# Page loads of the compression phase issued from three queues instead of two

## The reference, cut to what matters

```
def _compress(kv_rows, pe_k, w1_k, w2_k, pe_v, w1_v, w2_v, k_norm_g):
    idx = jnp.arange(n_cmp)[:, None] * CMP_STRIDE + jnp.arange(CMP_BLK)[None, :]
    blk = kv_rows[:, idx]
    def phi(x, pe, w1, w2):
        x = (x + pe[:, None, :]).transpose(0, 1, 3, 2, 4).reshape(B, n_cmp, NSA_GROUPS, CMP_BLK * HEAD_DIM)
        return jax.nn.gelu(x @ w1) @ w2
    kc = _rms(phi(blk[:, :, :, 0], pe_k, w1_k, w2_k), k_norm_g)
    vc = phi(blk[:, :, :, 1], pe_v, w1_v, w2_v)
```

## Time and profile before

| | us |
|---|---|
| median of 3 runs | 3017.89 (3014.96 to 3022.27) |
| the profiled execution, its own time | 3013.03 |
| its span in the profile | 3011.3 |
| the compression phase in it | about 463.5 to 704.9 |
| PE idle in that phase, waiting for rows | 14.4, 15.8 and 17.0 |

### The profile page before, as it was taken

One profiled execution on the slowest core, in us unless ns is written; L12 is line 12 of the kernel. 1 busy time (PEld: TensorE's weight loads), 2 busy tenths in 40 slices (PEclk: granted clock), 3 DMA queues, 4 the chain that ended last, 5 costly groups with the idle time before them and its releaser, 6 DMA issues.

```text
span 3011.3 us, 44556 instructions
## 1 busy us (share of the span) xinstructions
PE 2725.2 (90%) x18210; PEld 2239.4 (74%) x18210; DVE 934.6 (31%) x2644; ACT 640.0 (21%) x1615; POOL 482.5 (16%) x461
## 2 busy tenths in 40 slices
PE   7999994798998755997599999999999999999995
PEld 3555534544666544644599999999999999999995
DVE  1122121114766442145422223232322322232222
ACT  1111111114756410022011111111111111111111
POOL 0000002100000000012222313131322321222121
PEclk9999985898999866798799999999999999999997
DMA  5000026200000222321677778888889999999995
GB/s 183 11 21 20 13 92 155 56 0 27 1 1 1 82 74 84 105 84 55 245 245 245 254 262 273 282 285 301 294 294 321 316 313 326 318 322 309 324 317 176
DMA packets 278641, 533.63 MB, mean 177 GB/s; under 512 B 53906, under 2 KB 90226, under 8 KB 278226
## 3 DMA queue, kind: packets, MB, share of 16 engines
q1 hardware_dynamic: 234610, 475.29, 44.5%
q0 software_dynamic: 33120, 46.46, 7.2%
q10 hardware_dynamic: 10704, 9.00, 0.9%
HBM read 492.21 MB, written 42.96 MB: 178 GB/s over the span
## 4 chain that ended last, share of the span: by engine, by line
PE 50%; DMA 1%; DVE 1%; SPq 0%; issue 0%; POOL 0%; POOLq 0%; ACT 0%; DVEq 0%; ACTq 0%
PE up L2030 33%; PE down L2041 17%; DMA w_up<-summed_rows 0%; DMA slot_rows<-slot_tokens_gates 0%; DMA summed_rows<-y_rows,row_index_cur 0%; SPq L1978 0%; POOL summed_rows L1994 0%; PE down L2047 0%; POOLq L1874 0%; DVE nb L2162 0%; DVE hT L2119 0%; DVEq L1939 0%; DVE obt L2168 0%; DVE obt L2173 0%; DVE obf L2169 0%
## 5 line engine op out<-in xcount | busy, mean ns | idle before, releaser
L2030 PE MATMUL up<-hT,w_up 128*128 128x128 f32 (+19 forms) x8192 | 1008.0, 286 | 18.2 <-DVE hT L2119 18.2
L2030 PEld LDWEIGHTS up<-hT,w_up 128*128 128x128 f32 x8192 | 1004.9, 191 | 18.5 <-issue 18.5
L2041 PE MATMUL down<-actT,w_down 128*128 128x128 f32 (+19 forms) x4096 | 508.0, 286 | 0.5 <-DVE actT L2144 0.4
L2041 PEld LDWEIGHTS down<-actT,w_down 128*128 128x128 f32 x4096 | 503.6, 191 | 1.9 <-DVE actT L2144 0.9
L1994 POOL DMA_INDIRECT summed_rows<-y_rows,row_index_cur x153 | 241.0, 1575 | 1086.0 <-ACT y_rows L2060 1049.4
L2139 DVE TENSOR_SCALAR glu<-up,b_up_cur 128x128 f32<-128x128 f32 (+19 forms) x256 | 93.5, 365 | 1021.1 <-PE up L2030 1000.1
L305 PE MATMUL zp<-w_in,xnT 128*128 128x512 f32 (+3 forms) x896 | 366.0, 565 | 1.4 <-DVE xnT L479 1.4
L305 PEld LDWEIGHTS zp<-w_in,xnT 128*128 128x128 f32 (+1 forms) x896 | 156.8, 191 | 185.5 <-issue 181.5
L2071 ACT ACTIVATE sig<-glu 128x128 f32<-128x128 f32 (+19 forms) x256 | 82.4, 322 | 869.0 <-DVE glu L2139 797.0
L2079 ACT ACTIVATE yT<-down,b_down_cur 128x128 f32<-128x128 f32 (+19 forms) x256 | 97.2, 380 | 394.4 <-PE down L2041 394.4
L1988 POOL DMA_INDIRECT x_rows<-h_rows,row_index_cur x153 | 149.8, 979 | 65.1 <-issue 46.0
(11 more groups left out here) (389 smaller groups left out, 2089.6 us busy)
## 6 DMA issues: line engine op xcount, KB each, us to landing
w_up<-in_w_up SPq DMA_DIRECT2D x128, 2048.0 KB, 10.7
w_down<-in_w_down SPq DMA_DIRECT2D x64, 2048.0 KB, 8.0
w_in<-in_w_in SPq DMA_DIRECT2D x5, 2048.0 KB, 13.1
x<-in_cache_cmp_kv SPq DMA_DIRECT2D x80, 64.0 KB, 2.3
cache_rows<-in_cache_slc_kv SPq DMA_DIRECT2D x40, 128.0 KB, 3.1
x<-in_x_prompt SPq DMA_DIRECT2D x8, 512.0 KB, 3.6
window_rows<-in_cache_win_kv SPq DMA_DIRECT2D x8, 512.0 KB, 4.3
window_rows<-in_x_prompt SPq DMA_DIRECT2D x8, 512.0 KB, 3.9
```

The lines of the kernel that those rows point to most:

```text
L2030: mm = nc.tensor.matmul(up[c % 2][:, h, :N], U[c // 4][:, h, kk, w0:w0 + P], hT[:, kk, :N], start=(kk == 0), stop=(kk == KC - 1))
L2041: mm = nc.tensor.matmul(dn[d % 2][:, :N], Dn[:, kk // 4, kk % 4, d * P:d * P + P], aT[:, kk, :N], start=(kk == 0), stop=(kk == KC - 1))
```

## The change

The two sets of pages become three: of each sequence SP keeps pages 0, 3 and 6, POOL keeps 1, 4 and 7, and ACT gets 2 and 5 (`ACT_PAGES`). ACT issues its pages of source 1 in its own program behind its two copies of T(0,1), and those of source 2 behind its four copies of T(1,1). The prompt's eight transfers are split: SP issues the four of the even tokens, POOL the four of the odd ones. POOL no longer waits for `s_w[0]`. PE waits for one semaphore per queue. The diff, cut to its core:

```diff
+ACT_PAGES = (2, 5)
@@
-        s_xo = [None] + [sem(f"pool_pairs_loaded{j}") for j in range(2)]
+        s_xo = [sem(f"pool_pairs_loaded{j}") for j in range(3)]
+        s_xa = [None] + [sem(f"act_pairs_loaded{j}") for j in range(2)]
@@ the helpers
-        def load_pages(eng, gi, pool):
+        def load_pages(eng, gi, pages, semaphore):
...
-                for pg in range(PAGES):
-                    if (pg in POOL_PAGES) != pool:
-                        continue
+                for pg in pages:
...
+        def load_prompt(eng, r, semaphore):
+            prompt = o["cmp_p"].rearrange("l b (t m r) k g d -> (l b m) t r (k g) d", m=P, r=2)
+            for jt in range(4):
+                eng.dma_start(x2_of[0][:, 0, jt].rearrange("p a (r d) -> p r a d", r=2)[:, r], prompt[:, jt, r]).then_inc(semaphore[0], 16)
+
+        sp_pages = [pg for pg in range(PAGES) if pg not in POOL_PAGES + ACT_PAGES]
@@ SP
-            for jt in range(4):
-                for r in range(2):
-                    sp.dma_start(...).then_inc(s_x[0], 16)
-            load_pages(sp, 1, False)
+            load_prompt(sp, 0, s_x)
+            load_pages(sp, 1, sp_pages, s_x)
...
-            load_pages(sp, 2, False)
+            load_pages(sp, 2, sp_pages, s_x)
@@ POOL
-            pool.wait_ge(s_w[0], 32)
-            load_pages(pool, 1, True)
+            load_prompt(pool, 1, s_xo)
+            load_pages(pool, 1, POOL_PAGES, s_xo)
             pool.wait_ge(s_t, first_t[1, 1] + nT(1))
-            load_pages(pool, 2, True)
+            load_pages(pool, 2, POOL_PAGES, s_xo)
@@ ACT, after the copies of a "T"
+                if (op, gi, kv) == ("T", 0, 1):
+                    load_pages(act, 1, ACT_PAGES, s_xa)
+                if (op, gi, kv) == ("T", 1, 1):
+                    act.wait_ge(s_t, first_t[1, 1] + nT(1))
+                    load_pages(act, 2, ACT_PAGES, s_xa)
@@ PE
-                        pe.wait_ge(s_x[gi], 16 * (2 * nb * PAGES - npool if gi else 8))
+                        pe.wait_ge(s_x[gi], 16 * (2 * nb * len(sp_pages) if gi else 4))
+                        pe.wait_ge(s_xo[gi], 16 * (2 * nb * len(POOL_PAGES) if gi else 4))
                         if gi:
-                            pe.wait_ge(s_xo[gi], 16 * npool)
+                            pe.wait_ge(s_xa[gi], 16 * 2 * nb * len(ACT_PAGES))
```

More of the change, by code:

```diff
@@ L623, in load_pages @@
                     for r in range(2):
-                        eng.dma_start(dst[:, r], src[:, r]).then_inc((s_x, s_xo)[pool][gi], 16)
+                        eng.dma_start(dst[:, r], src[:, r]).then_inc(semaphore[gi], 16)
+        def load_prompt(eng, r, semaphore):
[3 more added lines that the diff above has]
+        sp_pages = [pg for pg in range(PAGES) if pg not in POOL_PAGES + ACT_PAGES]
         @block.sync
         def _(sp):
-            prompt = o["cmp_p"].rearrange("l b (t m r) k g d -> (l b m) t r (k g) d", m=P, r=2)
-            for jt in range(4):
-                for r in range(2):
-                    sp.dma_start(x2_of[0][:, 0, jt].rearrange("p a (r d) -> p r a d", r=2)[:, r], prompt[:, jt, r]).then_inc(s_x[0], 16)
-            load_pages(sp, 1, False)
+            load_prompt(sp, 0, s_x)
+            load_pages(sp, 1, sp_pages, s_x)
             for j, n in enumerate(("k", "v")):
@@ L687, in _ @@
                     if kv == 0:
-                        npool = 2 * nb * len(POOL_PAGES)
-                        pe.wait_ge(s_x[gi], 16 * (2 * nb * PAGES - npool if gi else 8))
+                        pe.wait_ge(s_x[gi], 16 * (2 * nb * len(sp_pages) if gi else 4))
+                        pe.wait_ge(s_xo[gi], 16 * (2 * nb * len(POOL_PAGES) if gi else 4))
                         if gi:
-                            pe.wait_ge(s_xo[gi], 16 * npool)
+                            pe.wait_ge(s_xa[gi], 16 * 2 * nb * len(ACT_PAGES))
                     for m in range(nT(gi)):
```

## The result

| | median us | runs | ratio to the kernel before | interval (95%) |
|---|---|---|---|---|
| before | 3015.28 | 6 | | |
| the change | 2993.22 | 6 | 0.9935 | 0.9919 to 0.9952 |

The change makes the kernel faster by about 20 us (0.65% of 3015.28; 14.5 to 24.4 by the interval). 2989.7 had been forecast, 28.2 us less than the median then known.

A forecast was written before the change was run, and what follows sets the result against it. PE was taken to be bound by waits for pages, from SP's late issuing and, early in source 1, full engines. Gains of 9.4 + 17.0 + 1.75 = 28.2 us from 3017.9 gave 2989.7; range 2982 to 3004.

The forecast's parts named there:

- What bounded the waits: PE's waits for pages, 15.8 and 17.0 us: SP's issuing at 1.073 us a step sets the end at source 2.
- The term was 18.75: Source 2: the 17.0 us wait before T(2,0) goes whole, and T(2,0) at full clock saves 1.75 us.
- Rival 2: SP and ACT slow each other in issuing; time 3010.2, or 3001 with half of that slowing; chance 0.11.
- At the 241 GB/s ... 4.9 us; I take 4.3: Source 1: 1.2 MB more from SP and POOL delays the second weight on ACT's queue by 4.3 us, bounds 0 and 10.
- ACT free at 488.4: Source 1: ACT gets through its constants at 488.4 instead of 484.1, then copies the prompt and issues pages.
- the 494: Sign of being wrong: ACT's copies of the prompt start after 494, where 486 to 490 was expected.
- rival 1: Source 1: ACT held by its constants until 494 or longer; gain 3.7 instead of 9.4, time 2995.4; chance 0.19.
- 9.4 were told: Source 1: PE's wait before T(1,0) shrinks from 15.8 to 6.4 us, 9.4 us less.
- PE gets the prompt's rows earlier, perhaps by 3 to 5 us: Start of the phase: splitting the prompt over SP and POOL brings its rows 3 to 5 us earlier, worth nothing.
- weights, which come no earlier: Start of the phase: the chain up to M(0,0) also needs the weights, and these come no earlier.
- nothing is added here: Source 1: PE's idle time stays long enough for the clock to fall as it did, so no clock gain.
- The rule against the change: Skill's rule that spreading saves only small issuing time: by it the waits stay and the time is 3017.9.

The follow-up runs named there:

- e_src2_two: Kernel before, with only source 2's pages shared anew: SP and POOL four of each sequence each, ACT none; 3009.2 us, ratio 0.9982.
- e_poolwait: Changed kernel, with POOL waiting again for the keys' weight and encodings, between its prompt transfers and its pages; 2988.5 us, ratio 0.9919.
- e_src1: Kernel before, with only the prompt and source 1 spread over the queues and POOL's wait gone; 3013.6 us, ratio 0.9997.
- e_wlate: Changed kernel, with ACT issuing the values' weight (2 MB) behind its pages of source 1; 2983.5 us, ratio 0.9893.
- e_petrans: Changed kernel, with position encodings loaded as 512-byte rows, each set behind its weight, and turned by PE and DVE; 2992.8 us, ratio 0.9927.
- e_both: Changed kernel, with the values' weight behind ACT's pages of source 1 and the encodings as rows with a transpose; 2982.2 us, ratio 0.9896.
- e_rows_first: Changed kernel, with the encodings as 512-byte rows issued ahead of both weights, then transposed; 2989.8 us, ratio 0.9913.

## Why the prediction was right or wrong

- **Direction and range: right.** 2993.2 lies in 2982 to 3004. The forecast of 28.2 us less was too large: 20 were measured, 24.4 at most by the interval, and the phase is 17.8 us shorter. That the time still came within 3.5 us of 2989.7 is in part luck: the kernel before has a median of 3015.3 over six runs where 3017.9 was known, and of the 23.3 us between the two profiled executions 5.5 arose outside the phase.
- **What bounded the waits: right for source 2.** 24 issues took 25.80 us on SP, and ACT's sixteen 16.22, both near the 1.073 a step that SP had shown. PE's wait was 0.59 us where under 2 was told, and T(2,0) ran at clock 1.00 in 584.30 - 579.64 = 4.7 us (4.5 forecast). The term was 18.75 and measured 18.0. e_src2_two shows the same rule with other numbers.
- **Rival 2, SP and ACT slowing each other in issuing: did not happen** with nothing else in the queues. Steps stayed at 1.07 while both issued. In source 1 SP's 24 did take 32.11 us instead of 25.8. With POOL's pages held back they took 26.49 (e_poolwait), so it came with POOL's early pages beside ACT's constants.
- **The step that failed: "At the 241 GB/s ... 4.9 us; I take 4.3", ACT free at 488.4.** It was free at 497.2, 8.8 later, and past the 494 that the prediction had named as a sign of being wrong. The bytes were not undercounted: 1.2 MB more from POOL and SP had been told, and 0.85 MB had come by 483.5, when the weight lands in the kernel before. The price was wrong. The sum let ACT's weight give way by those bytes at an unchanged total rate, but the total fell from 282 to 244 GB/s in these 20 us, and the weight landed 12.9 us later (496.6 for 483.7). The prediction also left out that the issue of the values' weight is itself held until the keys' weight has landed: it ended 3.6 us later (476.85 for 473.25). This is rival 1, which had 0.19, and worse than its 494; its clause that M(0,0) slips came true too. The wait shrank by 6.4 us where 9.4 were told, but M(0,0) ended 4.1 us later (507.2 for 503.1), so that only 2.3 us were left, 0.5 of them from ahead of the phase.
- **"PE gets the prompt's rows earlier, perhaps by 3 to 5 us": wrong in sign.** T(0,0) started 14.6 us after the phase's start, and 12.7 before. In e_poolwait it is 12.3, so it was POOL's pages, not the split of the prompt, that delayed it. **"weights, which come no earlier"** missed that they come later: the keys' encodings landed at 483.3 instead of 475.3.
- **"nothing is added here"** for the clock at source 1: in this profile what was left of the gain was lost there. The products of the values' encodings took 12.03 us instead of 10.16. By the granted clock of the stretches (0.71 from 520 to 528; before 0.91 from 522 to 524 and 0.93 from 524 to 530) PE ran at its upper level (2.4 GHz) for some 3.4 us there instead of 6.8, an estimate from these shares. It isn't so in every profile: in e_src1, with the same source 1, the products took 9.71 us and M(1,0) began 87.9 us after the phase's start, against 88.8 in the changed kernel and 88.5 before.
- **The rule against the change.** The Trainium skill ("DMA: Bandwidth & Descriptors", section "Issuing engines are not separate DMA queues") has it that several issuing engines save only the issuing time, usually small beside the transfer. At source 2 that saving was 18 us, so the measurement decides against "small". At source 1 spreading brought nothing (0.9997), but that doesn't bear the rule out: e_wlate spreads the same pages, only moves a weight behind them, and is 10 us faster than the change. What stood against the gain there was the load ahead of ACT's issues.

## What to carry to other kernels

Before spreading transfers over more queues, look at each wait by itself: where the last queue's issues times its step give the end and the engines are 30 to 50% busy, the gain was computed to a microsecond; where the engines are full and the new issuing engine has large loads ahead, it came to nothing here until one of the loads was moved. An engine that computes and also issues is a poor place for a page load behind large constants: look up how long its issues are held, and move what isn't needed yet (here a 2 MB weight) behind the loads that are. And if a gate between queues is removed, count what its traffic does to the transfers that it had protected.

## What the hardware showed that was not expected

- **Busy shares of the DMA engines don't add.** The pages of source 2 took 17.3 us of 16 engines' time from two queues. From three queues the share from 552 to 579 was 0.89, 24.0 us, for the same bytes, and landing rose from a median of 2.3 to 3.7 us on SP. Here the stretch row of the changed kernel:

```profile
552.00:579.00 27.00, 27.00 (x64) 11.83 (x63) 0.14 (x1) 2.26 (x3) 14.71 (x24) 1.00 0.89 156
```

- **An ACT issue waits while two transfers of 2048 pieces ahead of it haven't landed.** This fits within 1.5 us in every kernel here that has two such in ACT's queue. The bytes alone don't do it: in e_petrans and e_both the same 8 KB in the same place went as 16 rows, and the issue behind a weight and one set of encodings took 0.54 and 1.20 us instead of 10.54 (the change) and 10.71 (e_wlate). Here is that of e_both:

```profile
464.26 1.20 ACTq L657 DMA_DIRECT2D pe_rows<-in_cmp_pe_v  x1
```

  The number and the size of the pieces changed together, and no run separates them.
- **8 KB in 4-byte pieces took 19.8 to 24.6 us to land** with the change and in e_wlate, and 11 to 15 before. As 512-byte rows in the same places as in e_wlate they took 13.1 and 11.7 us where it had been 20.9 and 24.6 (e_both). Issued first of all they took 2.0 and 2.3 (e_rows_first). So the cutting and the place in the queue each have a share.
- Why the total rate fell when POOL's pages ran beside ACT's constants is open in part. Two runs narrow it: with POOL's pages held back (e_poolwait), or with the 4-byte pieces gone (e_petrans), more than half of the fall was gone. How the engines divide their time between the two isn't shown.
